# Second attention: probabilities times values as three rounded products over pairs of query tiles, with two rotation steps and the query's low part on GpSimd

## The reference, cut to what matters

```python
qx = apply_rope_2(rms_norm_2(split_heads(aq, 8, 128), q_norm), cos, sin)
kx = apply_rope_2(rms_norm_2(split_heads(ak, 2, 128), k_norm), cos, sin)
attn_x = gqa_attention(qx, concat([kx, kc]), concat([vx, vc]))
# in gqa_attention, for each head and each block of 128 queries:
s = einsum('bqhgd,bkhd->bhgqk', q_blk, k) * 128 ** -0.5
p = softmax(s, axis=-1)
o = einsum('bhgqk,bkhd->bqhgd', p, v)
```

## Time and profile before

| | |
|---|---|
| median of 3 runs | 1739.9 us (1738.98 to 1741.16) |
| span of the profiled execution, first to last instruction | 1735.4 us |
| own time of the profiled execution | not given; the median is 4.5 us above the span |
| TensorE busy | 98% |
| VectorE, ScalarE, GpSimd busy | 59%, 49%, 41% |
| loop of the second attention, turn(1) to turn(31) | 751.96 to 885.41 us |

### The profile page before, as it was taken

One profiled execution on the slowest core, in us unless ns is written; L12 is line 12 of the kernel. 1 busy time (PEld: TensorE's weight loads), 2 busy tenths in 40 slices (PEclk: granted clock), 3 DMA queues, 4 the chain that ended last, 5 costly groups with the idle time before them and its releaser, 6 DMA issues.

```text
span 1735.4 us, 24655 instructions
## 1 busy us (share of the span) xinstructions
PE 1692.2 (98%) x8729; PEld 1380.6 (80%) x8729; DVE 1015.5 (59%) x1600; ACT 842.2 (49%) x1472; POOL 703.9 (41%) x795
## 2 busy tenths in 40 slices
PE   8999999989999999999999999999999999999998
PEld 6877777767786667878888888887888888888887
DVE  5578785687558864376658757777534533222222
ACT  5465665787366654356542354565423431313131
POOL 2634444426542015311123432333345465555554
PEclk9999999999999999999999999999999999999999
DMA  7362624222231003201058511112233223333333
GB/s 224 110 190 78 191 89 116 91 86 83 79 89 44 21 13 88 61 25 37 25 165 262 180 52 47 50 37 61 61 91 92 84 86 97 98 97 97 97 97 109
DMA packets 217150, 160.55 MB, mean 93 GB/s; under 512 B 8333, under 2 KB 190614, under 8 KB 217046
## 3 DMA queue, kind: packets, MB, share of 16 engines
q1 hardware_dynamic: 201758, 125.50, 25.2%
q10 hardware_dynamic: 15288, 33.66, 5.7%
HBM read 156.98 MB, written 2.16 MB: 92 GB/s over the span
## 4 chain that ended last, share of the span: by engine, by line
PE 66%; issue 11%; DVE 8%; POOL 7%; ACT 7%; DMA 1%; ACTq 0%; POOLq 0%; SPq 0%; DVEq 0%
PE ps L666 14%; PE ps L670 14%; PE ps L667 14%; POOL wl L616 7%; PE ps L3192 3%; PE ps L3195 3%; PE ps L3193 3%; PE ps L2242 2%; DVE mod_late L2638 2%; PE ps L2224 2%; PE ps L1688 1%; PE ps L2231 1%; PE ps L2788 1%; ACT wh L629 1%; PE ps L1656 1%
## 5 line engine op out<-in xcount | busy, mean ns | idle before, releaser
L616 POOL TENSOR_TENSOR wl<-raw,wh 128x256 fp32r<-128x256 f32 (+1 forms) x775 | 680.5, 909 | 972.3 <-ACT wh L629 972.2
L666 PE MATMUL ps<-ah,wh 128*128 128x512 f32 (+1 forms) x1144 | 456.9, 399 | 5.3 <-DVE al L794 2.2
L670 PE MATMUL ps<-ah,wl 128*128 128x512 f32 (+1 forms) x1144 | 446.7, 391 | 0.2
L667 PE MATMUL ps<-al,wh 128*128 128x512 f32 (+1 forms) x1144 | 445.7, 390 | 0.0
L629 ACT ACTIVATE wh<-raw 128x1024 fp32r<-128x1024 f32 (+1 forms) x220 | 230.7, 1049 | 300.1 <-PE ps L670 143.2
L666 PEld LDWEIGHTS ps<-ah,wh 128*128 128x128 f32 (+1 forms) x1144 | 213.6, 187 | 58.5 <-issue 6.8
L670 PEld LDWEIGHTS ps<-ah,wl 128*128 128x128 f32 (+1 forms) x1144 | 213.4, 187 | 49.6 <-POOL wl L616 2.4
L667 PEld LDWEIGHTS ps<-al,wh 128*128 128x128 f32 (+1 forms) x1144 | 213.8, 187 | 43.8 <-issue 1.7
L666 PE MATMUL ps<-bh,wh 128*128 128x512 f32 (+1 forms) x332 | 133.8, 403 | 1.7 <-DVE bl L1494 1.6
L670 PE MATMUL ps<-bh,wl 128*128 128x512 f32 (+1 forms) x332 | 130.5, 393 | 0.8 <-POOL wl L616 0.7
L667 PE MATMUL ps<-bl,wh 128*128 128x512 f32 (+1 forms) x332 | 129.9, 391 | 0.0
(11 more groups left out here) (470 smaller groups left out, 2956.8 us busy)
## 6 DMA issues: line engine op xcount, KB each, us to landing
raw<-w_mlp SPq DMA_DIRECT2D x64, 512.0 KB, 3.9
raw<-w_in SPq DMA_DIRECT2D x52, 512.0 KB, 3.8
raw<-ssm_w_in SPq DMA_DIRECT2D x40, 512.0 KB, 4.0
ada_late<-w_ada ACTq DMA_DIRECT2D x16, 1024.0 KB, 7.1
ada_raw<-w_ada ACTq DMA_DIRECT2D x16, 512.0 KB, 4.5
cum_rows<-cum_saved ACTq DMA_DIRECT2D x16, 512.0 KB, 3.9
raw<-ssm_w_out SPq DMA_DIRECT2D x16, 512.0 KB, 3.4
raw<-mla_w_in SPq DMA_DIRECT2D x11, 512.0 KB, 3.9
```

The lines of the kernel that those rows point to most:

```text
L616: nc.gpsimd.tensor_tensor(wl[:, s, part], raw[:, s, part], wh[:, s, part].bitcast(F32), ALU.subtract).then_inc(lo_ready, LOW_PIECES * (par ...
L666: nc.tensor.matmul(dst, w_hi[k], x_hi[k], start=k == 0, stop=False)
L667: nc.tensor.matmul(dst, w_hi[k], x_lo[k], start=False, stop=False)
L670: ins = nc.tensor.matmul(dst, w_lo[k], x_hi[k], start=False, stop=k == n - 1)
```

## The change: what it does

- `outputs` works on a pair of query tiles (m = 0 to 15, 256 columns) and as three F32R products for each of the 6 key blocks: 18 matmuls of 256 columns where two tiles had 2 x 6 plain float32 products of 128 columns (24 records). It stands after the projection and ahead of turn(n), for even n, and waits until both tiles of the pair have their high and their low part.
- The turned probabilities are rounded into `g_turned_hi` by ScalarE (`copy_turned`, strided into its half of the pair; one pair buffer), and a new VectorE step `low_turned(n)` takes the rest from banks 6 and 7 into `g_turned_lo`. It is the first thing of VectorE's iteration n + 1. turn(n) now waits for `low_turned(n - 1)`, where it waited for copy_turned(n - 1).
- The values are split the same way ahead of the loop (`high_v` on ScalarE, `take_v` on VectorE).
- For heads 1 to 6 the two steps of `turned_q` and the one of `low_q` go from VectorE to GpSimd (`swing_q`), which does them between its weight units. VectorE's waits for them are added in `turn_q` and `scale_q`, and TensorE's in `scores`.
- Buffers move: `p_sq` and `v_lo` lie over norm buffers.

```diff
@@ tiles
-        v_tok = r("v_tok", [P, KT, KVH * HD])
+        v_hi, v_lo = r("v_hi", [P, KT, KVH * HD], F32R), at("v_lo", [P, KT, KVH * HD], F32R, norm_v_at)
-        g_probs_t = r("g_probs_t", [P, 2, KT, P])
+        PAIR = 2 * P
+        g_turned_hi = r("g_turned_hi", [P, KT, PAIR], F32R)
+        g_turned_lo = r("g_turned_lo", [P, KT, PAIR], F32R)
+        BY_POOL = range(1, QH - 1)
+        Q_STEPS = 4
+        V_PARTS = KT // 2
+        def swing_q(pool, j):
+            pool.wait_ge(sem("head_tables"), 2)
+            pool.wait_ge(sem("q_steps"), Q_STEPS * j - 3)
+            nc.gpsimd.tensor_tensor(p_sin[:], p_sin[:], head_cs[:, 0, 1], ALU.mult).then_inc(sem("q_steps"), 1)
+            pool.wait_ge(sem("q_steps"), Q_STEPS * j - 2)
+            pool.wait_ge(acc_free[0], ACC0["gqa"][0] + 2 * j + 2)
+            nc.gpsimd.tensor_tensor(p_cos[:], p_cos[:], p_sin[:], ALU.add).then_inc(sem("q_steps"), 1)
+            pool.wait_ge(sem("qk_high"), split_q_at(j))
+            nc.gpsimd.tensor_tensor(q_lo[:, j % 2], p_cos[:], q_hi[:, j % 2].bitcast(F32), ALU.subtract).then_inc(sem("q_steps"), 1)
@@ TensorE
             def turn_probs(n):
                 pe.wait_ge(sem("g_probs_ready"), n + 1)
-                pe.wait_ge(*((sem("g_copied"), n) if n else (sem("k_ln"), KVH)))
+                pe.wait_ge(*((sem("g_lowered"), V_PARTS + n) if n else (sem("k_ln"), KVH)))
-            def outputs(n):
-                j, t = divmod(n, TT)
-                pe.wait_ge(sem("g_copied"), n + 1)
-                if t == 0:
+            def outputs(m):
+                j, two = divmod(m, TT // 2)
+                pe.wait_ge(sem("g_copied"), V_PARTS + 2 * m + 2)
+                pe.wait_ge(sem("g_lowered"), V_PARTS + 2 * m + 2)
+                if two == 0:
                     pe.wait_ge(acc_free[1], ACC0["gqa"][1] + 1 + j + 1)
+                v, dst = slice(j // QPK * HD, (j // QPK + 1) * HD), bank(1)[:, two * PAIR:(two + 1) * PAIR]
                 for k in range(KT):
-                    ins_ = nc.tensor.matmul(bank(1)[:, t * P:(t + 1) * P], v_tok[:, k, v], g_probs_t[:, n % 2, k], start=k == 0, stop=k == KT - 1)
+                    nc.tensor.matmul(dst, v_hi[:, k, v], g_turned_hi[:, k], start=k == 0, stop=False)
+                    nc.tensor.matmul(dst, v_lo[:, k, v], g_turned_hi[:, k], start=False, stop=False)
+                    ins_ = nc.tensor.matmul(dst, v_hi[:, k, v], g_turned_lo[:, k], start=False, stop=k == KT - 1)
@@ TensorE, the loop
+                if n and n % 2 == 0:
+                    outputs(n // 2 - 1)
                 turn_probs(n)
-                if n:
-                    outputs(n - 1)
-            outputs(NQ - 1)
+            outputs(NQ // 2 - 1)
@@ ScalarE
             def copy_turned(n):
                 act.wait_ge(sem("g_turned"), n + 1)
-                if n >= 2:
-                    act.wait_ge(sem("g_o"), n - 1)
+                if n >= 2 and n % 2 == 0:
+                    act.wait_ge(sem("g_o"), n // 2)
...
@@ VectorE
             def low_q(j):
+                if j in BY_POOL:
+                    return
...
             def turned_q(j):
+                if j in BY_POOL:
+                    return
...
+            def low_turned(n):
+                dve.wait_ge(sem("g_copied"), V_PARTS + n + 1)
+                half = slice(n % 2 * P, (n % 2 + 1) * P)
+                nc.vector.tensor_tensor(g_turned_lo[:, :, half], ps[:, 6:8].rearrange("p b n -> p (b n)")[:, 0:TA].rearrange("p (k n) -> p k n", n=P),
+                                        g_turned_hi[:, :, half].bitcast(F32), ALU.subtract).then_inc(sem("g_lowered"), 1)
@@ VectorE, the loop
             for n in range(NQ):
                 j, t = divmod(n, TT)
+                if n:
+                    low_turned(n - 1)
                 if t == 1 and j:
                     low(j - 1)
                 if n + 1 < NQ:
...
+            low_turned(NQ - 1)
             low(QH - 1)
@@ GpSimd
                     for n in range(per):
+                        if stage == "gqa" and n > q_unit(2):
+                            swing_q(pool, n - q_unit(2))
                         split_low(pool, stage, i, n)
+                if stage == "gqa":
+                    swing_q(pool, QH - 2)
```

More of the change, by code:

```diff
@@ L331, in _build @@
         ada_loaded = [sem(f"ada_loaded{k}") for k in range(3)]
-        consts_in, rows_in, tokens_in, ready = sem("consts_in"), sem("rows_in"), [sem("tokens_in0"), sem("tokens_in1")], sem("ready")
+        consts_in, rows_in, tokens_in = sem("consts_in"), sem("rows_in"), [sem("tokens_in0"), sem("tokens_in1")]
         stage_done = sem("stage_done")
@@ L2071, in _build @@
         k_feat = r("k_feat", [P, KVH, TA])
-        v_tok = r("v_tok", [P, KT, KVH * HD])
-        p_sq = r("p_sq", [P, TA])
-        p_rstd = r("p_rstd", [P, TA])
+        v_hi, v_lo = r("v_hi", [P, KT, KVH * HD], F32R), at("v_lo", [P, KT, KVH * HD], F32R, norm_v_at)
+        p_sq = at("p_sq", [P, T], F32, norm_sq_at)
+        p_rstd = r("p_rstd", [P, T])
         p_cos = r("p_cos", [P, T])
@@ L2141, in _build @@
         split_q_at, split_k_at = (lambda j: j + (1, 2, 3)[min(j, 2)]), (lambda n: 2 * n + 2)
+        BY_POOL = range(1, QH - 1)
+        Q_STEPS = 4
+        V_PARTS = KT // 2
+        LOW_COUNT = {0: 2, QPK: 3, QH - 1: 4}
+        def swing_q(pool, j):
[7 more added lines that the diff above has]
+            nc.gpsimd.tensor_tensor(q_lo[:, j % 2], p_cos[:], q_hi[:, j % 2].bitcast(F32), ALU.subtract).then_inc(sem("q_steps"), 1)
         def pe_gqa(pe):
@@ L2161, in sum_k @@
                 pe.wait_ge(sem("k_squared"), 2 * n + 2)
-                pe.wait_ge(*((sem("k_ln"), n) if n else (sem("gv_taken"), 2)))
+                pe.wait_ge(*((sem("k_ln"), n) if n else (sem("g_lowered"), 2)))
                 nc.tensor.matmul(bank(6), ones[:], k_sq[n][:, 0:T], start=True, stop=True)
@@ L2212, in scores @@
                 if n == 0:
[L2213 to L2217, removed]
+                    pe.wait_ge(sem("g_lowered"), 3)
+                if t == 0:
+                    if j in BY_POOL:
+                        pe.wait_ge(sem("q_steps"), Q_STEPS * j)
+                    if j in LOW_COUNT:
+                        pe.wait_ge(sem("qk_low"), LOW_COUNT[j])
                 if n >= 2:
@@ L2336, in copy_turned, with high_v @@
                 act.wait_ge(sem("g_turned"), n + 1)
-                if n >= 2:
-                    act.wait_ge(sem("g_o"), n - 1)
-                nc.scalar.activation(g_probs_t[:, n % 2].rearrange("p k n -> p (k n)"), ps[:, 6:8].rearrange("p b n -> p (b n)")[:, 0:TA],
+                if n >= 2 and n % 2 == 0:
+                    act.wait_ge(sem("g_o"), n // 2)
+                nc.scalar.activation(g_turned_hi[:, :, n % 2 * P:(n % 2 + 1) * P],
+                                     ps[:, 6:8].rearrange("p b n -> p (b n)")[:, 0:TA].rearrange("p (k n) -> p k n", n=P),
+                                     ACT.Copy).then_inc(sem("g_copied"), 1)
+            def high_v(part):
+                act.wait_ge(*((sem("gv_projected"), part + 1) if part < 2 else (unit_done, unit("gqa", 0, 1) + 1 + CREDIT)))
+                nc.scalar.activation(v_hi[:, 2 * part:2 * part + 2], bank((6, 7, 3)[part]).rearrange("p (t d) -> p t d", t=2),
                                      ACT.Copy).then_inc(sem("g_copied"), 1)
             def high(j):
-                act.wait_ge(sem("g_o"), TT * (j + 1))
+                act.wait_ge(sem("g_o"), TT // 2 * (j + 1))
                 nc.scalar.activation(bh[:, j], bank(1), ACT.Copy).then_inc(sem("g_high"), 1)
@@ L2369, in act_gqa @@
                 split_ahead(act, "gqa", 0, half)
+            for part in range(3):
+                high_v(part)
             take_q(0)
@@ L2405, in dve_gqa, with turn @@
             st = dve_steps[0]
-            def turn(src, kind, dst, release):
-                st(nc.vector.stream_shuffle(p_sin[:], src, HALVES))
+            def turn(src, kind, dst, release, shuffled=st):
+                shuffled(nc.vector.stream_shuffle(p_sin[:], src, HALVES))
                 nc.vector.tensor_tensor(dst, src, head_cs[:, kind, 0], ALU.mult).then_inc(release, 1)
@@ L2443, in turn_q @@
                 dve.wait_ge(sem("q_squared"), j + 1)
-                if j:
-                    dve.wait_ge(sem("qk_low"), split_q_at(j - 1))
+                if j - 1 in BY_POOL:
+                    dve.wait_ge(sem("q_steps"), Q_STEPS * (j - 1))
+                elif j:
+                    dve.wait_ge(sem("qk_low"), 1)
                 st.wait()
-                turn(bank(0), 0, p_cos[:], acc_free[0])
+                if j in BY_POOL:
+                    turn(bank(0), 0, p_cos[:], acc_free[0], lambda ins_: ins_.then_inc(sem("q_steps"), 1))
+                else:
+                    turn(bank(0), 0, p_cos[:], acc_free[0])
             def turned_q(j):
+                if j in BY_POOL:
+                    return
                 turned(0, p_cos[:], acc_free[0], ACC0["gqa"][0] + 2 * j + 2)
@@ L2453, in scale_q @@
```

(11 more changed lines are left out.)

1 line of the change is left out of this document (removed).

## The result

The kernel after takes 1784.07 us (median of 4 runs, 1782.59 to 1784.65), beside 1739.44 for the kernel before in the same job (4 runs, 1737.54 to 1741.16): a ratio of 1.026, 95% interval 1.0248 to 1.0272. It is slower by 44.6 us; 26.7 was forecast. The profiled execution has a span of 1782.9 us, 47.5 more than before, and its own time is 1784.65, so that only 1.75 lies around the span.

A forecast was written before the change was run, and what follows sets the result against it. TensorE bounds the loop now; afterwards VectorE's list and the chain through banks 6 and 7 would. 15.8 + 4.8 + 1.6 + 4.5 = +26.7 on span 1735.4 gives 1762.1, plus 4.5: 1766 us, range 1755 to 1772 (0.68).

The forecast's parts named there:

- The chain: Loop: banks 6 and 7 pass turn, copy, low_turned, next turn, outputs ahead at even tiles; head 20.9 us, 2.4 above today's.
- heads 6 and 7: Six steps from turn(25) to turn(31): 27.3 us instead of 22.5, the chain showing more, +4.8.
- The sum, from turn to turn: Whole span: 15.8 to turn(25), 4.8 to turn(31), 1.6 at the end, 4.5 GpSimd beside VectorE, +26.7 us.
- the stretch ahead of turn(1): Before the loop: turn(1) moves because it waits for low_turned(0), at most 1.1 us, taken as 0.9.
- turn(1) to turn(25): Six heads: 125.8 us after the change instead of 110.95, before the separate GpSimd term.
- the end: From turn(31) to branch_a: 4.85 us instead of 3.25, +1.6.
- The contention term: GpSimd's new instructions beside VectorE's gained and scale at tile 3: nothing to some 14 us, taken as 4.5.
- the nearest row: Earlier collision in the profile: VectorE product 1.05 instead of 0.69 us, four GpSimd pieces 3.73 instead of 2.83.
- this rival: GpSimd holds VectorE off for its whole instructions, and the split of weights as well: 1772 to 1778, chance 0.15.
- The clock: Rival: clock falls because TensorE idles; at half, a head near 35 us and the time above 1850, chance 0.02.
- The offset: Median of the runs against the profiled span: 4.5 us above it, taking 1762.1 to 1766.

The follow-up runs named there:

- Experiment 1: Kernel after without low_turned and the product with the probabilities' low part, 12 matmuls a pair, turn waiting for the copy alone: 1741.91 us, ratio 1.0020.
- experiment 5: Kernel after with the 12 products of the high probabilities ahead of the wait for the low part: 1765.62 us, ratio 1.0144.
- experiment 3: Kernel after with the two gained (and stack_low) of each head moved from tile 3 to tile 2 on VectorE: 1760.36 us, ratio 1.0130.
- experiment 2: Kernel after with the two rotation steps and the query's low part back on VectorE, GpSimd only with weight units: 1769.70 us, ratio 1.0193.
- the second kernel of the last group: Kernel after, rotation on VectorE, high products before the low-part wait, low_turned behind top at tiles 0, 2, 3 of heads 0-5, gained at tile 2: 1744.59 us.

## Why the prediction was right in direction and wrong in size

**The chain: right.** Even tiles were forecast at 4.9 us and tile 1 at 4.8; after has 4.94 (810.19 to 815.13) and 4.82 (805.37 to 810.19) at tiles 2 and 1 of head 2, and in the other heads the same to 0.02, but for tile 2 of head 0 (5.57) and for tile 1 of head 1, where the keys add what was forecast (6.04), and of heads 0 and 7, which lack a step (4.2). VectorE's wait at the start of an even tile's low part was forecast at 1.3 and is 1.25. `low_turned` was scaled from `k_lo` to 0.96 and takes 0.954 in the mean, the new matmuls step by 0.12 at 2.4 GHz, heads 6 and 7 cost 5.2 (27.7 us from turn(25) to turn(31) instead of 22.5) against 4.8. Experiment 1 shows that nearly all of the loss hangs on the low part, experiment 5 that the chain can be shortened where the prediction drew it.

**The sum, from turn to turn.** Of the span's +47.5, the stretch ahead of turn(1) has 4.2 (forecast 0.9), turn(1) to turn(25) has 35.4 (146.3 instead of 110.95; forecast 14.9 + 4.5), turn(25) to turn(31) 5.2 (4.8), the end 2.9 (1.6). The miss in spans, 20.8, is thus 16 in the six heads (contention 5.5 more than was taken, the clock 10.6, which was put at nothing), 3.3 ahead of them, 0.4 in heads 6 and 7 and 1.3 at the end. The term that failed most is the clock's.

**The contention term: mis-sized.** "By the slowdown of the nearest row", I took 4.5 between 0 and 14. It was about 10, nearer to the upper end: `gained` 3.13 instead of 1.41 and the scale 1.15 instead of 0.62, with tile 3 at 8.4 in heads 0 to 3 and 7.4 in head 4, where 6.3 was forecast. The nearest row had GpSimd pieces of 0.7 us, and each could hold a VectorE instruction off for its rest only; the new ones take 1.26 and more. The Trainium skill (SBUF — State Buffer, "Who interferes with whom") calls the port pair that VectorE and GpSimd share an exclusive lock: the order of issue decides who is blocked. For two SBUF inputs it says only that they contend; blocking for the other's whole instruction it states for VectorE's 2-port modes (one tensor read through both ports). The rows agree with whole instructions here too: GpSimd's instructions end at 821.41 and 823.08, and the `gained` that starts while each of them runs ends 0.55 us behind it, at 821.97 and 823.63. The first loses 0.7 us by that, the second 1.0, and GpSimd's second is itself 1.59 instead of 1.29. By the same section a VectorE instruction with at most one input in SBUF is spared, outside those modes, as `low_turned` was in experiment 3. I had given this rival 0.15, because the row was milder.

**The clock: a rival with the wrong shape.** I had asked whether the clock falls for the whole loop, answered with the average of one window (3.92 of 5 us busy at 1.00) and gave it 0.02. The sum has every term at full clock. What happens is partial. At tile 0 TensorE waits 1.5 us ahead of `sum_q`, works 1.1 and waits again, 2.9 us in heads 1 to 4 and 1.9 in head 5, and the clock is at 1.2 GHz for the work behind that. Tile 0 then takes 6.5 to 7.4 us instead of 4.9 in heads 1 to 5, 10.6 in all; it is 4.99 in head 6 (896.38 to 901.37), where the two waits are 1.2 us each and the clock held. The same happens ahead of turn(1), where the new GpSimd steps delay the first turn from 748.03 to 750.32 (it is at 747.93 in experiment 2, without them), and behind the last wait. After's window around turn(1):

```profile
752.00:756.00 4.00, 4.00 (x12) 3.17 (x11) 2.61 (x4) 2.08 (x6) 0.00 (x0) 0.50 0.00 0
```

And TensorE's timeline at the end, where the clock falls within the last outputs (0.12 a step, then 0.21), which is the end's other 1.3 us:

```profile
932.99 0.36 PE L2262 MATMUL ps<-g_turned_hi,v_hi 128*128 128x256 f32 x1 [1.99 <-DVE g_turned_lo L2507]
...
933.66 0.28 PE L2264 MATMUL ps<-g_turned_lo,v_hi 128*128 128x256 f32 x1
933.78 0.35 PE L2262 MATMUL ps<-g_turned_hi,v_hi 128*128 128x256 f32 x1
...
935.86 0.41 PE L2263 MATMUL ps<-g_turned_hi,v_lo 128*128 128x256 f32 x1
936.07 0.41 PE L2264 MATMUL ps<-g_turned_lo,v_hi 128*128 128x256 f32 x1
```

The two misses feed each other. TensorE has only scores and `sum_q` at tile 0, and waits there for a low part that the blocked `gained` has made late; with `gained` at its normal length (experiments 2 and 3) the second wait is 1.2 us or none, and the clock mostly holds. So one reorder gave 24 us, more than its own 4 x 1.7: the clock's 10 us come with it, and tile 3's list is shorter by `gained` itself, which tile 2 takes up in a wait.

**The offset.** I added 4.5 us from span to median. The time stands 1.8 above the span in the profiled executions of after and of every experiment. The first medians of before came from runs other than the profiled one. By luck this hid 2.7 us of the miss.

**Left open.** All variants keep a wait of `sum_q` for VectorE's cosine product at tile 0, 4.7 us in the second kernel of the last group; moving `sum_q` was not tried. What decides whether the clock falls is open as well: the length of the waits does not tell it. Two waits of 1.6 and 1.2 us were followed by half clock in one head of experiment 2 and by full clock in four, and a single wait of 2.2 us in tile 2 of head 6 left the clock alone in after and was followed by 1.2 GHz in experiment 3.

## What to carry to other kernels

Before a step goes into a chain around a buffer that exists once, list what each engine has queued around it, and look for the place where that engine already waits: behind `top`, `low_turned` takes up 0.86 us of a wait of 1.06, until the list turns into a circle. Work moved to GpSimd is not free even with a head of slack: ask which VectorE instructions with two operands in SBUF start while it runs, and price the collision by GpSimd's whole instruction. And where a change makes TensorE wait, list the waits one by one with the work between them, and give the work right behind a cluster of them a case of its own at half clock (here 1.5 to 2.5 us a tile); the busy share of the whole head (17.7 of 21 us) hid it.

## What the runs showed of the hardware that was not expected

- Two waits of 1.5 and 2.9 us with 1.1 us of work between them were followed by 1.2 GHz over all or nearly all of the next 3.7 to 4 us, in a loop where TensorE waited 0.4 us in all before; 84 useless matmuls made the kernel 6.4 us faster.
- The same pair of shorter waits (some 1.6 and 1.2 us) was followed by 1.2 GHz in one head and by 2.4 in others of one execution.
- VectorE's scale (one tensor in SBUF, a column of factors) took 1.15 us instead of 0.62 beside GpSimd's pieces of 256 columns, though it has one tensor input only; `low_turned`, with an operand in PSUM, kept its 0.94 beside a GpSimd instruction of 1.27.
- The same 128x512 operation on two tensors takes GpSimd 1.26 to 1.30 us and VectorE 0.69 when neither is disturbed.
